# Stand-in products at the waits of every looped expert block, three more in the router heads, and overflow registers loaded before the last block

## What is computed

```python
p_group = softmax(t @ w_group + b_group); g_w, g_idx = top_k(p_group, 1)
e_w, e_idx = top_k(softmax(e_logits of that group), 2)          # 8 groups x 8 experts
combine = ... weights of the two experts of each token
for e in range(64):
    hid = silu(t @ w_gate[e]) * (t @ w_up[e])                   # w_gate, w_up: 1024 x 256
    acc += combine[:, e, None] * (hid @ w_down[e])              # w_down: 256 x 1024
```

## Time and profile before

| | |
|---|---|
| median of 3 runs | 1582.69 us (1580.06 to 1584.27) |
| the profiled execution | 1584.61 us |
| its span, first to last instruction | 1582.9 us |
| mean granted TensorE clock | 0.941 |
| PE busy | 1369.5 us, 87% |
| DVE, ACT, POOL busy | 609.6, 264.7, 105.0 us |
| transfers | 512.68 MB, mean 324 GB/s |

### The profile page before, as it was taken

The page is one execution under the profiler, slowest core; times in us unless marked ns, Lnnn a source line. Parts: engine busy times, 40 slices in busy tenths (PEclk is TensorE's granted clock), DMA queues, the critical chain, the costliest instruction groups (busy, mean ns, idle before and its releaser), DMA issues.

```text
span 1582.9 us, 24259 instructions
## 1 busy us (share of the span) xinstructions
PE 1369.5 (87%) x9338; PEld 830.3 (52%) x9338; DVE 609.6 (39%) x1504; ACT 264.7 (17%) x736; POOL 105.0 (7%) x191
## 2 busy tenths in 40 slices
PE   9999998776776779989998766766779999999997
PEld 4455655433433444556564433433445875988843
DVE  3774542221221222862633221221213553677721
ACT  2143211100010011362111100100101042111100
POOL 1312000000000001211000000000001051000000
PEclk9999999988988989999999888988989999999999
DMA  8878599999999999729699999999999952644300
GB/s 301 309 293 297 225 422 420 421 421 422 422 422 422 422 422 389 263 87 410 283 421 420 421 421 422 422 422 422 422 422 382 377 176 69 197 148 159 133 0 27
DMA packets 120372, 512.68 MB, mean 324 GB/s; under 512 B 12000, under 2 KB 46748, under 8 KB 69096
## 3 DMA queue, kind: packets, MB, share of 16 engines
q1 hardware_dynamic: 118576, 507.50, 80.7%
q0 software_dynamic: 1552, 4.06, 0.8%
q10 hardware_dynamic: 168, 0.09, 0.0%
HBM read 510.54 MB, written 1.07 MB: 323 GB/s over the span
## 4 chain that ended last, share of the span: by engine, by line
PE 37%; DMA 12%; SPq 6%; issue 1%; DVE 1%; ACT 1%; POOL 0%; ACTq 0%; POOLq 0%; DVEq 0%
DMA ring<-in_moe_w_up 10%; PE bank L2311 10%; SPq L1704 6%; PE bank L2342 5%; PE bank L1287 4%; PE bank L2057 3%; PE bank L537 2%; DMA BC<-in_moe_w_up 2%; PE bank L429 2%; PE bank L441 2%; PE bank L1274 1%; PE bank L1302 1%; PE bank L1316 1%; PE bank L682 1%; PE bank L705 1%
## 5 line engine op out<-in xcount | busy, mean ns | idle before, releaser
L1287 PE MATMUL bank<-ring,hT 128*32 128x256 f32 (+1 forms) x2976 | 303.7, 467 | 133.5 <-DMA ring<-in_moe_w_up 53.2
L1287 PEld LDWEIGHTS bank<-ring,hT 128*32 128x32 f32 (+1 forms) x2976 | 162.2, 135 | 245.2 <-issue 181.1
L1553 DVE TENSOR_SCALAR pT<-pT 128x256 f32<-128x256 f32 x34 | 10.0, 294 | 457.8 <-ACT pT L1671 457.8
L1287 PE MATMUL bank<-BC,hT 128*32 128x256 f32 x1056 | 137.8, 427 | 46.3 <-DMA ring<-in_moe_w_up 35.3
L2311 PE MATMUL bank<-hT,ring 128*128 128x256 f32 (+1 forms) x768 | 152.9, 362 | 0.0
L2311 PEld LDWEIGHTS bank<-hT,ring 128*128 128x128 f32 x768 | 135.9, 190 | 16.5
L1274 PE MATMUL bank<-A,hn 128*128 128x128 f32 x1088 | 128.8, 277 | 0.1
L1274 PEld LDWEIGHTS bank<-A,hn 128*128 128x128 f32 x1088 | 126.1, 194 | 0.2
L1302 PE MATMUL bank<-ring,gtab 128*32 128x512 f32 (+1 forms) x768 | 123.6, 595 | 0.9 <-ACT gtab L1665 0.9
L537 PE MATMUL bank<-ring,hT 128*128 128x512 f32 (+4 forms) x352 | 121.7, 507 | 0.3 <-DVE hT L308 0.2
L1316 PE MATMUL bank<-hT,A 128*128 128x512 f32 x256 | 118.4, 605 | 0.0
(11 more groups left out here) (307 smaller groups left out, 1564.0 us busy)
## 6 DMA issues: line engine op xcount, KB each, us to landing
ring<-in_moe_w_up SPq DMA_DIRECT2D x98, 1024.0 KB, 26.8
ring<-in_moe_w_down SPq DMA_DIRECT2D x88, 1024.0 KB, 26.3
ring<-in_moe_w_gate SPq DMA_DIRECT2D x88, 1024.0 KB, 25.7
BC<-in_moe_w_gate SPq DMA_DIRECT2D x40, 1024.0 KB, 23.3
BC<-in_moe_w_down SPq DMA_DIRECT2D x32, 1024.0 KB, 26.5
BC<-in_moe_w_up SPq DMA_DIRECT2D x26, 1024.0 KB, 26.2
ring<-in_w_ada SPq DMA_DIRECT2D x24, 1024.0 KB, 12.9
ring<-in_w_up SPq DMA_DIRECT2D x22, 1024.0 KB, 5.3
```

The source lines that it names most:

```text
L1287: i = nc.tensor.matmul(GATE[q * cap:(q + 1) * cap, part * FF:(part + 1) * FF], xg[:, c, q * cap:(q + 1) * cap], u[:, c, :], start=(c == 0) ...
```

## The change

It issues the 6 and 9 stand-in products in the looped blocks as well as in the last one (not in the four written-out ones), seven stand-ins instead of four in each router head, and moves the load of the overflow register on PE, DVE and ACT ahead of the last block; the branch stays behind it. POOL also waits for ACT's last rows.

```diff
@@ tensor, router head
-                stand_in(4)
+                stand_in(7)
@@ tensor, block
                     for part in range(2):
-                        if following is None:
+                        if following is None or i is not None:
                             keep_warm(pe, 7, NB, (6, 9)[part])
                         for q in range(n):
                             here(u0 + part * n + q)
@@ tensor, behind the loop
-                block(BLOCKS - 1, 3 * E - 12, QUAD, None)
-
                 pe.wait_ge(*overflow(1))
                 over = pe.value_load(over_i[0:1, 0:1], min_val=0, max_val=S)
+                block(BLOCKS - 1, 3 * E - 12, QUAD, None)
+
                 with pe.If(over > 0):
@@ vector, behind the loop
+                dve.wait_ge(*overflow(1))
+                over = dve.value_load(over_i[0:1, 0:1], min_val=0, max_val=S)
                 block(BLOCKS - 1, 3 * E - 12, QUAD, None)
 
-                over = dve.value_load(over_i[0:1, 0:1], min_val=0, max_val=S)
@@ gpsimd
                 pool.wait_ge(*rows_v(BLOCKS))
+                pool.wait_ge(*rows_a(BLOCKS))
                 over = pool.value_load(over_i[0:1, 0:1], min_val=0, max_val=S)
```

## The result

The changed kernel takes 1677.57 us (median of 4 runs, 1676.27 to 1678.98) against 1582.49 us before on the same chip: 95.1 us more, a ratio of 1.0595 with a 95% interval of 1.058 to 1.0609. The profiled execution took 1676.27 us, with a span of 1674.6 and a mean granted clock of 0.993.

The account below looks back on a forecast made before the run. The prediction took weight transfers at 422 GB/s to pace the expert loops, with TensorE becoming the bound after the change. 72.2 + 7.6 + 0.9 - 1.5 = +79.2 us gave 1661.9 against the median, called 1661; range 1648 to 1671.

Parts of the forecast that it names:

- The loops' work: Expert loops: stand-ins make TensorE the bound at 31.65 us a block, 36.1 us lost per layer, +72.2 us in all.
- The stops: Loop branches back: the bigger body is no longer held, so TensorE stops four times at 1.9 us, +7.6 us.
- rival (a): Loop branches back: the larger body is still held, no stops, +71.6 us, 1654.3 us; chance 0.32.
- Heads and ends: Three more stand-ins per router head, +0.9 us; overflow registers loaded ahead of the last block, -1.5 us.
- The third block: The unedited code after the second expert layer: the prediction had no term for it, so 0.
- From execution to median: Profiled execution of the kernel before taken as 1.9 us above its median, so 1663.8 became 1661.9 us.
- Rival (d): Loops: more stops, at each new instruction block or late-freed slot, 61 us at most; a quarter gives 1677; chance 0.07.
- Rival (b): Loops: stand-ins absorbed, transfers stay the bound below 11.44 us of products a block, 1582.1 us; chance 0.04.
- Rival (c): Loops: 3.2 us of half clock a block come back, 77 us over 24 blocks, 1506 us; chance 0.01.

Follow-up runs that it names:

- experiment 7: The changed kernel with 4 and 6 full-width stand-ins in the looped blocks instead of 6 and 9: 1581.76 us, ratio 0.9988 to the kernel before.
- experiment 11: The changed kernel with 5 and 7 full-width stand-ins in the looped blocks instead of 6 and 9: 1618.86 us, ratio 1.0221 to the kernel before.
- experiment 6: The changed kernel with looped stand-ins 64 columns wide instead of 512, code length unchanged: 1588.07 us, ratio 1.0030 to the kernel before.
- experiment 1: The kernel before plus only the stand-ins in the looped blocks, heads and overflow loads unchanged: 1683.62 us, ratio 1.0634.
- experiment 4: The changed kernel with the looped blocks' stand-ins issued from two small loops (1 + 5 and 1 + 8 times): 1674.54 us, ratio 1.0581 to the kernel before.
- experiment 5: The kernel before plus 15 stand-ins per looped block, all ahead of the ups, one written out and fourteen from a small loop: 1645.12 us, ratio 1.0387.
- experiment 3: The kernel before plus only the overflow register loads moved ahead of the last block, with POOL's added wait: 1583.60 us, ratio 0.9995.
- experiment 2: The kernel before with seven stand-ins instead of four in each router head, nothing else: 1580.92 us, ratio 0.9985.
- experiment 10: The kernel of experiment 5 plus nine more stand-ins in each router head, shifting the loop in the instruction stream: 1669.01 us, ratio 1.0548 to the kernel before.
- experiment 8: The kernel before with seven stand-ins in the heads and 3 and 4 full-width ones in the last block, the others 64 columns: 1575.93 us, ratio 0.9950.
- experiment 9: The kernel before with seven stand-ins in the heads and 3 and 6 full-width ones in the last block, the others 64 columns: 1575.41 us, ratio 0.9949.

## Why the prediction was wrong

The direction, the cause and the largest term were right; the time, 1677.57 us, lies 16.6 above the forecast of 1661 and 6.6 above the range. By its steps:

- **The loops' work** was forecast at 31.65 us a block and +72.2 us. It measured 31.63 to 31.65 a block, and the two loops' 46.8 + 42.4 less the stops of the next point are 72.2. A price taken from the block that already ran at full clock held to 0.1%. Experiments 7 and 11 show the limit from both sides: ten products cost nothing, twelve do.
- **The stops are the term that was mis-sized.** The prediction said: "I take the upper end" with "four times 1.9 = 7.6 us". That there would be a stop at each of the four branches back, with fetches in every pass, was right, against rival (a). But they measured 13.6 us of idle time and 3.4 us lost to the half clock behind two of them, 17.0 in all: 9.4 more than forecast. The one row that I had, 3,909 ns, was no upper bound. The four branches back took 4.8 to 5.9 us after the change, and 6.0 to 6.4 in the kernels that keep the transfers at 418 to 420 GB/s (experiments 6, 7 and 11). The clock behind the stop stood in the earlier trace rows, 5.37 us for eight products that take 3.6, and I counted it as a possible gain at the overflow branch but not as a price at the others. The Trainium skill (Runtime: NRT & Kernel Launch, Instruction fetch mechanics) has the size by which I took the head for gone, 2,048 instructions for TensorE, refilled in blocks of 256, and the traces agree with it: the changed kernel and experiments 1, 4, 6, 7 and 11, whose bodies touch eight blocks or more, stop at every branch back, and the kernel before and experiment 5, with seven, at none. They don't agree with the window of two such pages that the same section gives a taken branch.
- **Heads and ends**: forecast +0.9 and -1.5. Measured +0.6 (-0.35 and +0.9) and -1.35. The end's size is right by luck: the stop didn't shorten, it grew from 2.20 to 2.50 us, and the gain is the clock that was kept behind it (the eight products took 3.67 us in place of 5.37). Experiment 3 shows that the load's place is worth nothing in the median. The head's step held; but whether the stop at the overflow branch is there, which is worth 2 to 4 us, changed in experiment 2 with an edit far ahead of it, and no term stood for that.
- **The third block** was forecast at 0 and took 3.25 us more. Over the thirteen kernels, in all of which its code is the same, the stretch from the second layer's last rows' product to the last matmul takes 361.9 to 366.7 us, with no order by what was edited but with one by the granted clock. It takes 361.9 to 362.0 where the clock stays at 1.00 (experiments 4, 5 and 7), 363.2 to 363.5 with 3.4 us at 0.50 (before, experiments 1 and 2), 364.7 with twice that (3), 365.0 with one stretch of 6.8 us (10), and 366.6 to 366.7 with 3.4 and 6.8 us (the changed kernel, experiments 6, 8, 9 and 11). So the 3.25 us are the 6.8 us at half clock that the changed kernel has from 1358.0 us on and the one of before hasn't. What makes the clock fall there in one kernel and not in another is open, and it limits what any such small term can be forecast to.
- **From execution to median**: the profiled execution of before lies 2.1 us above the median of its group, that of the changed kernel 1.3 below its own. The prediction subtracted the first and couldn't know the second: 3.4 us together.
- Together: 9.4 + 3.25 + 3.4, less 0.2 for heads and ends and 0.2 between the two medians of before, plus the 0.9 by which I rounded 1661.9 down, are the 16.6 us.

Rival (d), more and longer stops, gave 1677 at a quarter of its price. The time is right and the mechanism isn't: straight code in later passes runs without a stop; each of the four stops is longer, and there are no others. Rival (b) would have been right below 10.28 us of products a block (experiment 7), and the threshold of 11.44 that it named was wrong by the first block's share. Rival (c) fell: experiment 7 has the clock at 0.98 and no gain.

## What to carry to other kernels

Before filling idle time, ask what sets the period: time to spare is the measured length of the whole loop less the engine's own work, and filler is free up to there and at full price beyond. Count a loop's body in blocks of the instruction buffer and not in instructions, from where it begins; when it touches one block more than is held, every pass stops at its branch, and a small loop around repeated products can bring it back. And where weights have already come, a stand-in is nothing but delay: shortening them in the block behind the loops took the ratio from 0.9985 (experiment 2) to 0.9950.

## What the runs showed of the hardware

- TensorE's code came in blocks of 16 KB, 256 instructions. A loop that touched seven of them ran its later passes with no fetch and branches of 76 to 233 ns; at eight, with the next one fetched ahead, each pass was fetched anew (9 packets from branch to branch against none) and the branch back took 4.8 to 6.4 us, of which 2.9 to 4.5 were idle time (2.2 and 2.6 at the second of two in a row). The exception is a body that ends 6 instructions into the eighth block, which ran without a stop and without a fetch in the execution that was profiled.
- In the changed kernel the stops of 3.48 and 3.85 us in the first layer were each followed by 3.4 us at a granted clock of 0.50, and those of 2.86 and 3.40 in the second by none, behind the same instructions. The length of the stop doesn't settle it: in experiment 4 the clock fell behind all four, of 3.1 to 3.4 us.
- With 12 instructions added 450 us earlier in the stream a stop of 2.2 us was gone at a branch that nobody had edited (experiments 2, 8 and 9), and with the same instructions in the same places it was there in the changed kernel and not in experiment 6. Differences of 2 to 3 us between two versions of such a kernel can be that and nothing else.
